# Forget-gate logits as 8-column fp32 products in four column stripes of the PE array

## Chip, cores and metric

One core of one Trainium2 chip runs the whole program. The metric is the device time of one execution in microseconds; a kernel's time is the median over several executions.

## What is computed

Two transformer-like blocks run one after the other on 512 tokens of width 2048. Only the beginning of the first block matters here: one projection `x @ w_in`, of which eight columns are the forget-gate logits, one for each head. They go through a log-sigmoid and a running sum, and the sum enters the attention logits.

```python
proj = jnp.einsum('bsd,de->bse', x, w_in[l])
(q, k, v, g_att, fg, c_b, c_c, c_h, g_conv, p_u, g_pool) = jnp.split(proj, IN_SPLITS, axis=-1)
# in forgetting_attention:
log_f = jax.nn.log_sigmoid(fg_logit.astype(jnp.float32) + b_f.astype(jnp.float32))
cum = jnp.cumsum(log_f, axis=1)
...
logits = logits + cb[..., None] - cum_k[:, :, None, :]
```

## The kernel before

x is held transposed in `feats`, as 16 planes of 128 features by 512 tokens. Every projection is done at reduced operand width (fp32r) in three products: ACT rounds each operand to a high part (`planes_hi`, `w_hi`), DVE (for planes) or POOL (for weights) subtracts it from the raw value to get the low part (`planes_lo`, `w_lo`), and PE adds hi*hi, hi*lo and lo*hi in one PSUM bank. A tile is 128 output columns; it has 16 k-steps, so 48 matmuls, and its weights come in two units of 128x1024 (8 k-steps each). Units travel through four slots (`raw[:, s]`, `w_hi[:, s]`, `w_lo[:, s]`): SP issues the load, ACT rounds (`round_unit`, L843 is its ACTIVATE), POOL subtracts (`low_part`, L396, a tensor_sub with two SBUF inputs), PE multiplies. The semaphores `hi_ready`, `lo_ready` and `unit_used` count units through these stages. Each engine runs its instructions in the order in which the program lists them, so all that follows is an order written out by hand.

The start is special. The tile that PE meets first (`project_first`, ahead of the loop over tiles) uses slots 2 and 3, and its weight low parts are made by DVE (`first_low`, L1318), not POOL. While the planes still land from memory, ACT makes one high plane after the other (`cut_hi`, L889) and DVE one low plane after the other (`cut_lo`, L1267, also a subtraction of two SBUF operands); PE waits on `planes_ready` for each. In the same loop PE computes the forget-gate logits into bank M: `fg_w` holds, for each k-step, 128 stationary columns of which columns 0 to 7 are the rounded weights and 32 to 39 their low parts, the rest zero. It lies in slots 0 and 1 of `w_hi`, which POOL clears first, so that the units of tile 1 can be rounded into these slots only when PE has passed k-step 7 (slot 0) and k-step 15 (slot 1). Two matmuls a k-step are spent on it, 32 in all, beside the 48 of the tile.

The logits then leave M: ACT adds the bias (L922, into `tmp`), DVE copies the low part (L1338), adds it (L1340), takes min(x, -x) (L1256 into `gate`), ACT does Exp and Ln (L925, L926), DVE combines and scans (L1346) into `cumT`. These ACT steps stand ahead of the rounding of tile 2's first unit in ACT's order, and POOL's low part of that unit, which PE needs for tile 2, comes after it. Tile 1 is what PE computes meanwhile.

Of the kernel before, what the change touches and what calls it, by code (L numbers as in the profile page):

```python
# [27 lines left out]
P = 128  # L28
S = 512
D = 2048  # L30
QB = S // P
KT = D // P
UNIT = 1024
UK = UNIT // P
HEADS = 8
# [33 lines left out]
X_CUTS = [(0, 1), (1, 2)] + [(k, k + 2) for k in range(2, KT, 2)]  # L69
# [46 lines left out]
def block_kernel(nc, x_t, x_rows, w_fg, stream, params, pool_w, ln1, ln2, rope_idx, rope_qk, out):  # L116
    fp32, fp32r = mybir.dt.float32, mybir.dt.float32r
    ACT, ALU, AX = mybir.ActivationFunctionType, mybir.AluOpType, mybir.AxisListType.X
# [5 lines left out]
    with ExitStack() as ctx:  # L124
# [3 lines left out]
        def sem(name):  # L128
            return ctx.enter_context(nc.semaphore(name))


        planes_hi = sb("planes_hi", [P, KT, S], fp32r)
        planes_lo = sb("planes_lo", [P, KT, S], fp32r)
        feats = sb("feats", [P, KT, S])
        raw_at = nc.sbuf_base
        raw = sb("raw", [P, 4, UNIT])
        w_hi = sb("w_hi", [P, 4, UNIT], fp32r)
# [13 lines left out]
        probs = sb("probs", [P, QB, S])  # L151
# [38 lines left out]
        states = wide[:, 1024:2048].rearrange("p (c f) -> p c f", c=QB)  # L190
        resid = [bias, probs]
        fg_raw = vN[:, 0, 0, :].rearrange("p (k c) -> p k c", k=KT)
        fg_w = w_hi[:, 0:2, :].rearrange("p s (k c) -> p (s k) c", c=P)

        def end_slot(blk, v):

# [52 lines left out]
        hi_ready, lo_ready, unit_used = sem("hi_ready"), sem("lo_ready"), sem("unit_used")  # L249
        acc_taken = sem("acc_taken")  # L250
        x_loaded = [sem(f"x_loaded{c}") for c in range(len(X_CUTS))]
        fg_loaded, fg_zeroed = sem("fg_loaded"), sem("fg_zeroed")
        first_hi, first_ready = sem("first_hi"), sem("first_ready")
        half_loaded, warm_set = sem("half_loaded"), sem("warm_set")
        par_loaded, poolw_loaded = sem("par_loaded"), sem("poolw_loaded")
# [52 lines left out]
        def _(sp):  # L308
            def load(m, s):
                sp.dma_start(raw[:, s, :], stream[at(4 * m + s - 2), :, :].rearrange("u p n -> p (u n)"))\  # L310
                    .then_inc(raw_loaded[s], 16)
# [13 lines left out]
                load_x(c)  # L325
            load(1, 0)
            load(1, 1)
            sp.wait_ge(first_ready, 3)
            load(1, 2)
            sp.wait_ge(first_ready, 4)  # L330
            load(1, 3)
            def load_next(m, s):
                sp.wait_ge(lo_ready, 4 * m + s - 7)
# [38 lines left out]
        def _(pool):  # L372
# [3 lines left out]
                step(nc.gpsimd.affine_select(out=ap, in_=ap, compare_op=op, fill=fill, base=base,  # L376
                                             pattern=pattern, channel_multiplier=mult))

            nc.gpsimd.memset(w_hi[:, 0:2, :].bitcast(fp32), 0.0).then_inc(fg_zeroed, 1)
            step(nc.gpsimd.memset(ident[:, :], 0.0))  # L380
            select(ident[:, :], ALU.not_equal, 1.0, 0, [[-1, P]], 1)
            step(nc.gpsimd.memset(causal, 0.0))
# [58 lines left out]
        def _(pe):  # L441
            def mm(o, a, b, start=True, stop=True):
                return nc.tensor.matmul(o, a, b, start=start, stop=stop)  # L443
# [4 lines left out]

            def project_first():

                pe.wait_ge(first_ready, 2)
                for e in range(KT):
                    u, k = divmod(e, UK)
                    if e in (4, UK):
                        pe.wait_ge(first_ready, 3 if e < UK else 4)
                    pe.wait_ge(planes_ready, e + 1)
                    hi, lo = w_hi[:, 2 + u, P * k:P * k + P], w_lo[:, 2 + u, P * k:P * k + P]
                    mm(M[:, :], fg_w[:, e, :], planes_hi[:, e, :], e == 0, False)
                    fg_last = mm(M[:, :], fg_w[:, e, :], planes_lo[:, e, :], False, e == KT - 1)
                    if k == UK - 1:  # L460
                        fg_last.then_inc(unit_used, 1)
                    mm(ACC[1][:, :], hi, planes_hi[:, e, :], e == 0, False)
                    mm(ACC[1][:, :], hi, planes_lo[:, e, :], False, False)
                    last = mm(ACC[1][:, :], lo, planes_hi[:, e, :], False, e == KT - 1)
                last.then_inc(unit_used, 2)

            def project(tile, acc_before, planes_cut=None, after={}):
# [88 lines left out]

            pe.wait_ge(warm_set, 1)
            for _ in range(14):
                mm(O[:, 0:P], blank, blank)
            project_first()  # L560
            pe.wait_ge(consts, 1)
            project(tile_at(T_HEAD1, 1), None)
# [264 lines left out]
        def _(act):  # L827
            step = Steps(act, act_steps)

            def signal(ins, s, value):  # L830
                ins.then_inc(s, 1)
                act.wait_ge(s, value)

            def round_first(u, cols, loaded, value):

                act.wait_ge(loaded, 16)
                signal(nc.scalar.activation(w_hi[:, 2 + u, cols], raw[:, 2 + u, cols], ACT.Copy), first_hi, value)
# [20 lines left out]
            def turn_round(tile):  # L858

                m, p = tile  # L860
                for u in range(2):
                    round_unit(m + 1, 2 * p + u)
# [29 lines left out]
            def cut_early(blk, first):  # L892
# [3 lines left out]
                for n in range(EARLY):  # L896
                    cut_hi(BACK_ORDER[blk][n], 16 + 32 * blk + n + 1)

            act.dma_start(fg_raw, w_fg).then_inc(fg_loaded, 16)
            act.dma_start(feats[:, 0:1, :], x_t[:, 0:1, :]).then_inc(x_loaded[0], 16)  # L900
            act.dma_start(par[:, :], params).then_inc(par_loaded, 16)
            act.wait_ge(warm_set, 1)
            step(nc.scalar.activation(table_of[:, :], blank[:, 0:1], ACT.Copy))
            act.wait_ge(fg_zeroed, 1)
            act.wait_ge(fg_loaded, 16)
            signal(nc.scalar.activation(fg_w[:, :, 0:HEADS], fg_raw, ACT.Copy), first_hi, 1)
            round_first(0, slice(0, S), half_loaded, 2)
            for c, (k0, k1) in enumerate(X_CUTS):
                act.wait_ge(x_loaded[c], 16)
                for k in range(k0, k1):  # L910
                    cut_hi(k, k + 1)
                if c == 2:
                    round_first(0, slice(S, UNIT), raw_loaded[2], 3)
                if c == 4:
                    round_first(1, slice(0, UNIT), raw_loaded[3], 4)
            act.wait_ge(par_loaded, 16)
            turn_round((0, 0))
            xs = tmp[0:HEADS, :]
            ls = gate[0:HEADS, :]

            act.wait_ge(unit_used, 2)
            signal(nc.scalar.activation(xs, M[0:HEADS, :], ACT.Identity,  # L922
                                        bias=par[0:HEADS, PC["b_f"]:PC["b_f"] + 1]), acc_taken, 1)
            act.wait_ge(fg_turn, 1)
# [322 lines left out]
        def _(dve):  # L1247
            V = nc.vector
            step = Steps(dve, dve_steps)

            def signal(ins, s, value):
                ins.then_inc(s, 1)
                dve.wait_ge(s, value)
# [62 lines left out]
            def first_low(u, cols, value):  # L1316
                dve.wait_ge(first_hi, value)
                signal(V.tensor_sub(w_lo[:, 2 + u, cols], raw[:, 2 + u, cols], w_hi[:, 2 + u, cols].bitcast(fp32)),  # L1318
                       first_ready, value)

            V.memset(blank, 0.0).then_inc(warm_set, 1)
            dve.wait_ge(first_hi, 1)
            signal(V.tensor_sub(fg_w[:, :, 32:32 + HEADS], fg_raw, fg_w[:, :, 0:HEADS].bitcast(fp32)), first_ready, 1)
            first_low(0, slice(0, S), 2)
            cut_lo(0, 1)
            for k in range(1, 4):
                cut_lo(k, k + 1)
            first_low(0, slice(S, UNIT), 3)
            for k in range(4, UK):
                cut_lo(k, k + 1)  # L1330
            first_low(1, slice(0, UNIT), 4)
            for k in range(UK, KT):
                cut_lo(k, k + 1)
            xs, ls = tmp[0:HEADS, :], gate[0:HEADS, :]
            fg_low = probs[0:HEADS, 1, :]

            dve.wait_ge(unit_used, 2)
            step(V.tensor_copy(fg_low, M[32:32 + HEADS, :]))  # L1338
            dve.wait_ge(acc_taken, 1)
            step(V.tensor_add(xs, xs, fg_low))  # L1340
            signal(stt(ls, xs, -1.0, xs, MULT, MIN), fg_turn, 1)
            dve.wait_ge(consts, 1)
            step(V.memset(probs[0:HEADS, 0, :], 1.0))
# [540 lines left out]
```

## Time and profile before

| | us |
|---|---|
| median of 3 runs (lowest, highest) | 1733.69 (1732.19, 1733.84) |
| the profiled execution, its time | 1734.07 |
| the profiled execution, its span | 1732.3 |
| PE busy | 1714.9 (99%) |
| DVE busy | 725.8 (42%) |
| ACT busy | 590.0 (34%) |
| POOL busy | 696.2 (40%) |

The profile is of one execution. Its span is 1.8 us shorter than its time; a step that moves the span moves the time by as much. PE is TensorE's matmul, PEld its weight load, DVE is VectorE, ACT is ScalarE, POOL is GpSimd, SP the queue that issues most loads. One fp32 matmul is two records in the trace (two passes), one fp32r matmul is one. The times of timeline rows are counted from the start of the span. A matmul's duration in a row contains its latency through the array; what it costs a busy PE is the distance to the next start.

### The profile page before, as it was taken

The page shows a single profiled execution, that of the slowest core. Times are in us where ns is not written, and L with a number is a line of the kernel's source. Part 1 is how long each engine was busy: PE and PEld are TensorE (multiplying, and loading weights), DVE is VectorE, ACT ScalarE, POOL GpSimd, SP SyncE. Part 2 cuts the span into 40 slices and gives each one's busy share as a digit, 9 for nine tenths or more (in the row PEclk, how much of TensorE's full clock was granted, in tenths as well). Part 3 has the DMA queues.
Part 4 walks back from the last instruction along what each step waited for, and adds up shares of the span by engine and source line. Part 5 has one row for each costly group of instructions (what it writes and reads, how often), then busy time and mean ns, then how long its engine had stood idle before and what let it go on. Part 6 is the DMA issues. An engine that isn't in the chain of part 4 may idle for free.

```text
span 1732.3 us, 21500 instructions
## 1 busy us (share of the span) xinstructions
PE 1714.9 (99%) x7910; PEld 1392.9 (80%) x7910; DVE 725.8 (42%) x1222; ACT 590.0 (34%) x803; POOL 696.2 (40%) x301
## 2 busy tenths in 40 slices
PE   9999999999999999999999999999999999999997
PEld 7888888888888888888888888887568787788886
DVE  4223311232211134211662744748679734465226
ACT  5433323333222224212652333423452434362120
POOL 4433333433444444445243433334236333325451
PEclk9999999999999999999999999999999999999999
DMA  6432232332332332543254443434123222227332
GB/s 223 121 91 87 90 92 92 91 92 85 92 97 97 97 98 85 171 121 98 74 196 123 124 130 91 129 109 122 49 74 98 86 73 73 85 61 267 122 97 97
DMA packets 56221, 186.15 MB, mean 107 GB/s; under 512 B 5928, under 2 KB 6184, under 8 KB 55376
## 3 DMA queue, kind: packets, MB, share of 16 engines
q1 hardware_dynamic: 46512, 160.19, 30.1%
q10 hardware_dynamic: 9632, 24.88, 4.1%
q8 instruction: 55, 0.90, 0.2%
q14 instruction: 22, 0.18, 0.0%
HBM read 176.57 MB, written 8.47 MB: 107 GB/s over the span
## 4 chain that ended last, share of the span: by engine, by line
PE 94%; DVE 3%; issue 1%; ACT 1%; DMA 1%; POOL 0%; ACTq 0%; SPq 0%; DVEq 0%; POOLq 0%
PE bank L443 92%; PE bank L447 2%; POOL w_lo L396 0%; DVE feats L1256 0%; DVE padded L1512 0%; DMA probsT<-decay_dram 0%; ACT w_hi L843 0%; DVE probs L1513 0%; DVE probs L1514 0%; DMA feats<-in_x_t 0%; DVE padded L1511 0%; DVE planes_lo L1454 0%; DVE kT L1613 0%; DVE wide L1622 0%; DVE bank L1447 0%
## 5 line engine op out<-in xcount | busy, mean ns | idle before, releaser
L396 POOL TENSOR_TENSOR w_lo<-raw,w_hi 128x1024 fp32r<-128x1024 f32 x272 | 661.6, 2434 | 994.8 <-ACT w_hi L843 994.8
L443 PE MATMUL bank<-planes_hi,w_hi 128*128 128x512 f32 (+1 forms) x1792 | 708.5, 395 | 2.0 <-DVE planes_lo L1267 1.3
L443 PE MATMUL bank<-planes_lo,w_hi 128*128 128x512 f32 (+1 forms) x1792 | 691.1, 386 | 0.0
L443 PE MATMUL bank<-planes_hi,w_lo 128*128 128x512 f32 (+1 forms) x1776 | 685.6, 386 | 0.0
L843 ACT ACTIVATE w_hi<-raw 128x1024 fp32r<-128x1024 f32 x276 | 292.7, 1060 | 975.2 <-PE bank L443 940.1
L443 PEld LDWEIGHTS bank<-planes_hi,w_hi 128*128 128x128 f32 x1792 | 337.0, 188 | 86.9 <-issue 19.2
L443 PEld LDWEIGHTS bank<-planes_lo,w_hi 128*128 128x128 f32 x1792 | 337.2, 188 | 70.4 <-issue 5.3
L443 PEld LDWEIGHTS bank<-planes_hi,w_lo 128*128 128x128 f32 x1776 | 333.8, 188 | 68.2
L443 PE MATMUL bank<-w_hi,planes_hi 128*128 128x512 f32 x480 | 187.9, 392 | 0.0
L443 PE MATMUL bank<-w_hi,planes_lo 128*128 128x512 f32 x480 | 186.8, 389 | 0.0
L443 PE MATMUL bank<-w_lo,planes_hi 128*128 128x512 f32 x480 | 186.8, 389 | 0.0
L1299 DVE COPY probsT<-bank 128x512 f32<-128x512 f32 (+1 forms) x64 | 31.4, 491 | 184.1 <-PE bank L447 182.4
L443 PEld LDWEIGHTS bank<-w_lo,planes_hi 128*128 128x128 f32 x480 | 90.1, 188 | 19.2 <-issue 0.5
L443 PEld LDWEIGHTS bank<-w_hi,planes_hi 128*128 128x128 f32 x480 | 90.1, 188 | 19.0 <-issue 0.2
L443 PEld LDWEIGHTS bank<-w_hi,planes_lo 128*128 128x128 f32 x480 | 90.1, 188 | 18.7
L1308 DVE TENSOR_TENSOR feats<-bank,gate 128x512 f32 (+1 forms) x16 | 11.1, 692 | 148.8 <-PE bank L443 148.8
L1368 DVE TENSOR_TENSOR padded<-kT,vT 128x512 f32<-128x512 f32 x4 | 9.2, 2301 | 117.6 <-ACT gate L868 117.6
L1256 DVE SCALAR_TENSOR_TENSOR feats<-probs,bank 128x512 f32<-128x512 f32 x16 | 11.0, 688 | 93.6 <-PE bank L443 93.4
L1267 DVE TENSOR_TENSOR planes_lo<-feats,planes_hi 128x512 fp32r<-128x512 f32 x48 | 43.1, 898 | 15.3 <-ACT planes_hi L889 13.7
L1256 DVE SCALAR_TENSOR_TENSOR feats<-bias,bank 128x512 f32<-128x512 f32 x16 | 11.0, 687 | 86.9 <-PE bank L443 86.5
L875 ACT ACT_TABLE_LOAD x35 | 44.9, 1283 | 1.1 <-ACT vT L868 0.5
L881 ACT ACTIVATE probs<-probs,nmax 128x128 f32<-128x128 f32 (+1 forms) x64 | 36.0, 563 | 12.1 <-DVE nmax L1286 8.0
(262 smaller groups left out, 1247.5 us busy)
## 6 DMA issues: line engine op xcount, KB each, us to landing
raw<-in_stream SPq DMA_DIRECT2D x281, 512.0 KB, 3.6
h_rows<-feats ACTq DMA_DIRECT2D x4, 1024.0 KB, 7.1
feats<-in_x_t SPq DMA_DIRECT2D x7, 512.0 KB, 8.8
out<-feats ACTq DMA_DIRECT2D x7, 512.0 KB, 2.7
rope_q<-cum_dram ACTq DMA_DIRECT2D x8, 256.0 KB, 3.1
bias<-in_x_rows ACTq DMA_DIRECT2D x2, 1024.0 KB, 6.6
probs<-in_x_rows ACTq DMA_DIRECT2D x2, 1024.0 KB, 8.8
rope_q<-decay_dram SPq DMA_DIRECT2D x8, 256.0 KB, 5.3
```

What stands on the lines that cost most here:

```text
L396: nc.gpsimd.tensor_sub(w_lo[:, s, :], raw[:, s, :], w_hi[:, s, :].bitcast(fp32)).then_inc(lo_ready, 1)
L443: return nc.tensor.matmul(o, a, b, start=start, stop=stop)
L447: return nc.tensor.transpose(o, a, ident[0:k, 0:k])
L843: signal(nc.scalar.activation(w_hi[:, s, :], raw[:, s, :], ACT.Copy), hi_ready, 4 * m + s - 3 if value is None else value)
L875: step(nc.scalar.activation(table_of[:, :], ones[:, 0:1], func))
L881: signal(nc.scalar.activation(probs[:, i, 0:n], probs[:, i, 0:n], ACT.Exp, bias=nmax[:, i:i + 1], scale=-1.0, accum_out=rowsum[:, i:i + 1] ...
L1256: return V.scalar_tensor_tensor(out=o, in0=a, scalar=scalar, in1=b, op0=op0, op1=op1)
L1267: signal(V.tensor_sub(planes_lo[:, k, :], feats[:, k, :], planes_hi[:, k, :].bitcast(fp32)), planes_ready, value)
L1299: ins = V.tensor_copy(probsT[:, j, P * j:S], B[j][:, P * j:S])
L1308: signal(V.tensor_mul(feats[:, at(tile), :].rearrange("p a n -> p (a n)"), src[:, :], gate[:, :]), feat_done, count)
L1368: step(V.tensor_mul(padded[:, 16:16 + S], kT[:, 0, :], vT[:, :]))
```

## The change

The eight columns are no longer computed from rounded parts. PE multiplies the raw fp32 weights (`fg_raw`, 128 rows by 8 columns a k-step) with the raw fp32 planes (`feats`). The four k-steps of a group of four planes write to four different column stripes of the array, partitions 0, 32, 64 and 96 of M, so each stripe collects every fourth k-step. After k-steps 3, 7, 11 and 15 PE issues one such group of four fp32 matmuls of 8 columns by 512. DVE copies the three sums at partitions 32, 64 and 96 to partition 0 and adds them to ACT's biased first sum: three copies and three additions for one of each. The padded weight array, its rounding, its low part and POOL's clearing of it go. Slots 0 and 1 of `w_hi` are free from the start, and ACT rounds tile 1's first unit ahead of the last two planes and its second unit right behind them. ACT's queue issues the load of x's first plane ahead of that of the eight columns. The semaphore values move accordingly.

```diff
@@ -190,7 +190,6 @@
         states = wide[:, 1024:2048].rearrange("p (c f) -> p c f", c=QB)
         resid = [bias, probs]
         fg_raw = vN[:, 0, 0, :].rearrange("p (k c) -> p k c", k=KT)
-        fg_w = w_hi[:, 0:2, :].rearrange("p s (k c) -> p (s k) c", c=P)
 
         def end_slot(blk, v):
 
@@ -249,7 +248,7 @@
         hi_ready, lo_ready, unit_used = sem("hi_ready"), sem("lo_ready"), sem("unit_used")
         acc_taken = sem("acc_taken")
         x_loaded = [sem(f"x_loaded{c}") for c in range(len(X_CUTS))]
-        fg_loaded, fg_zeroed = sem("fg_loaded"), sem("fg_zeroed")
+        fg_loaded, fg_done = sem("fg_loaded"), sem("fg_done")
         first_hi, first_ready = sem("first_hi"), sem("first_ready")
         half_loaded, warm_set = sem("half_loaded"), sem("warm_set")
         par_loaded, poolw_loaded = sem("par_loaded"), sem("poolw_loaded")
@@ -325,9 +324,9 @@
                 load_x(c)
             load(1, 0)
             load(1, 1)
+            sp.wait_ge(first_ready, 2)
+            load(1, 2)
             sp.wait_ge(first_ready, 3)
-            load(1, 2)
-            sp.wait_ge(first_ready, 4)
             load(1, 3)
             def load_next(m, s):
                 sp.wait_ge(lo_ready, 4 * m + s - 7)
@@ -376,7 +375,6 @@
                 step(nc.gpsimd.affine_select(out=ap, in_=ap, compare_op=op, fill=fill, base=base,
                                              pattern=pattern, channel_multiplier=mult))
 
-            nc.gpsimd.memset(w_hi[:, 0:2, :].bitcast(fp32), 0.0).then_inc(fg_zeroed, 1)
             step(nc.gpsimd.memset(ident[:, :], 0.0))
             select(ident[:, :], ALU.not_equal, 1.0, 0, [[-1, P]], 1)
             step(nc.gpsimd.memset(causal, 0.0))
@@ -448,20 +446,24 @@
 
             def project_first():
 
-                pe.wait_ge(first_ready, 2)
+                pe.wait_ge(first_ready, 1)
                 for e in range(KT):
                     u, k = divmod(e, UK)
                     if e in (4, UK):
-                        pe.wait_ge(first_ready, 3 if e < UK else 4)
+                        pe.wait_ge(first_ready, 2 if e < UK else 3)
                     pe.wait_ge(planes_ready, e + 1)
                     hi, lo = w_hi[:, 2 + u, P * k:P * k + P], w_lo[:, 2 + u, P * k:P * k + P]
-                    mm(M[:, :], fg_w[:, e, :], planes_hi[:, e, :], e == 0, False)
-                    fg_last = mm(M[:, :], fg_w[:, e, :], planes_lo[:, e, :], False, e == KT - 1)
-                    if k == UK - 1:
-                        fg_last.then_inc(unit_used, 1)
                     mm(ACC[1][:, :], hi, planes_hi[:, e, :], e == 0, False)
                     mm(ACC[1][:, :], hi, planes_lo[:, e, :], False, False)
                     last = mm(ACC[1][:, :], lo, planes_hi[:, e, :], False, e == KT - 1)
+                    if e % 4 == 3:
+                        if e == 3:
+                            pe.wait_ge(fg_loaded, 16)
+                        for j in range(4):
+                            part = mm(M[32 * j:32 * j + HEADS, :], fg_raw[:, e - 3 + j, :], feats[:, e - 3 + j, :],
+                                      e == 3, e == KT - 1)
+                            if e == KT - 1:
+                                part.then_inc(fg_done, 1)
                 last.then_inc(unit_used, 2)
 
             def project(tile, acc_before, planes_cut=None, after={}):
@@ -556,7 +558,8 @@
 
             pe.wait_ge(warm_set, 1)
             for _ in range(14):
-                mm(O[:, 0:P], blank, blank)
+                warm = mm(O[:, 0:P], blank, blank)
+            warm.then_inc(unit_used, 2)
             project_first()
             pe.wait_ge(consts, 1)
             project(tile_at(T_HEAD1, 1), None)
@@ -896,29 +899,28 @@
                 for n in range(EARLY):
                     cut_hi(BACK_ORDER[blk][n], 16 + 32 * blk + n + 1)
 
+            act.dma_start(feats[:, 0:1, :], x_t[:, 0:1, :]).then_inc(x_loaded[0], 16)
             act.dma_start(fg_raw, w_fg).then_inc(fg_loaded, 16)
-            act.dma_start(feats[:, 0:1, :], x_t[:, 0:1, :]).then_inc(x_loaded[0], 16)
             act.dma_start(par[:, :], params).then_inc(par_loaded, 16)
             act.wait_ge(warm_set, 1)
             step(nc.scalar.activation(table_of[:, :], blank[:, 0:1], ACT.Copy))
-            act.wait_ge(fg_zeroed, 1)
-            act.wait_ge(fg_loaded, 16)
-            signal(nc.scalar.activation(fg_w[:, :, 0:HEADS], fg_raw, ACT.Copy), first_hi, 1)
-            round_first(0, slice(0, S), half_loaded, 2)
+            round_first(0, slice(0, S), half_loaded, 1)
             for c, (k0, k1) in enumerate(X_CUTS):
                 act.wait_ge(x_loaded[c], 16)
                 for k in range(k0, k1):
                     cut_hi(k, k + 1)
                 if c == 2:
-                    round_first(0, slice(S, UNIT), raw_loaded[2], 3)
+                    round_first(0, slice(S, UNIT), raw_loaded[2], 2)
                 if c == 4:
-                    round_first(1, slice(0, UNIT), raw_loaded[3], 4)
+                    round_first(1, slice(0, UNIT), raw_loaded[3], 3)
+                if c == len(X_CUTS) - 2:
+                    round_unit(1, 0)
+            round_unit(1, 1)
             act.wait_ge(par_loaded, 16)
-            turn_round((0, 0))
             xs = tmp[0:HEADS, :]
             ls = gate[0:HEADS, :]
 
-            act.wait_ge(unit_used, 2)
+            act.wait_ge(fg_done, 4)
             signal(nc.scalar.activation(xs, M[0:HEADS, :], ACT.Identity,
                                         bias=par[0:HEADS, PC["b_f"]:PC["b_f"] + 1]), acc_taken, 1)
             act.wait_ge(fg_turn, 1)
@@ -1319,25 +1321,23 @@
                        first_ready, value)
 
             V.memset(blank, 0.0).then_inc(warm_set, 1)
-            dve.wait_ge(first_hi, 1)
-            signal(V.tensor_sub(fg_w[:, :, 32:32 + HEADS], fg_raw, fg_w[:, :, 0:HEADS].bitcast(fp32)), first_ready, 1)
-            first_low(0, slice(0, S), 2)
+            first_low(0, slice(0, S), 1)
             cut_lo(0, 1)
             for k in range(1, 4):
                 cut_lo(k, k + 1)
-            first_low(0, slice(S, UNIT), 3)
+            first_low(0, slice(S, UNIT), 2)
             for k in range(4, UK):
                 cut_lo(k, k + 1)
-            first_low(1, slice(0, UNIT), 4)
+            first_low(1, slice(0, UNIT), 3)
             for k in range(UK, KT):
                 cut_lo(k, k + 1)
             xs, ls = tmp[0:HEADS, :], gate[0:HEADS, :]
-            fg_low = probs[0:HEADS, 1, :]
-
-            dve.wait_ge(unit_used, 2)
-            step(V.tensor_copy(fg_low, M[32:32 + HEADS, :]))
+            dve.wait_ge(fg_done, 4)
+            for j in range(1, 4):
+                step(V.tensor_copy(probs[0:HEADS, j, :], M[32 * j:32 * j + HEADS, :]))
             dve.wait_ge(acc_taken, 1)
-            step(V.tensor_add(xs, xs, fg_low))
+            for j in range(1, 4):
+                step(V.tensor_add(xs, xs, probs[0:HEADS, j, :]))
             signal(stt(ls, xs, -1.0, xs, MULT, MIN), fg_turn, 1)
             dve.wait_ge(consts, 1)
             step(V.memset(probs[0:HEADS, 0, :], 1.0))
```

## Rows read from the trace of the kernel before

**Rows 1.** The page: the span and the busy time of each engine.
```profile
span 1732.3 us, 21500 instructions
...
PE 1714.9 (99%) x7910; PEld 1392.9 (80%) x7910; DVE 725.8 (42%) x1222; ACT 590.0 (34%) x803; POOL 696.2 (40%) x301
```

**Rows 2.** The chain that ended last, first 60 us: start, us, what.
```profile
7.55 17.73 PE bank L443 x77
```

**Rows 3.** Timeline of PE, first tiles: start, us, engine, line, operation, idle before.
```profile
25.78 0.39 PE L443 MATMUL bank<-planes_hi,w_hi 128*128 128x512 f32 x1
...
36.44 0.39 PE L443 MATMUL bank<-planes_hi,w_lo 128*128 128x512 f32 x1
37.19 0.47 PE L443 MATMUL bank<-planes_hi,w_hi 128*128 128x512 f32 x1 [0.36 <-POOL w_lo L396]
```

**Rows 4.** Timeline of ACT, first 40 us.
```profile
13.36 5.28 ACT L889 ACTIVATE planes_hi<-feats 128x512 fp32r<-128x512 f32 x8
18.68 1.06 ACT L843 ACTIVATE w_hi<-raw 128x1024 fp32r<-128x1024 f32 x1
...
26.44 0.68 ACT L922 ACTIVATE tmp<-bank,par 8x512 f32<-8x512 f32 x1
```

**Rows 5.** Timeline of DVE, first 40 us.
```profile
6.71 2.95 DVE L1267 TENSOR_TENSOR planes_lo<-feats,planes_hi 128x512 fp32r<-128x512 f32 x4
...
14.61 5.78 DVE L1267 TENSOR_TENSOR planes_lo<-feats,planes_hi 128x512 fp32r<-128x512 f32 x8
25.37 0.68 DVE L1338 COPY probs<-bank 8x512 f32<-8x512 f32 x1 [4.98 <-PE bank L443]
27.23 2.20 DVE L1340 TENSOR_TENSOR tmp<-tmp,probs 8x512 f32<-8x512 f32 x1 [1.17 <-ACT tmp L922]
29.46 0.68 DVE L1256 SCALAR_TENSOR_TENSOR gate<-tmp 8x512 f32<-8x512 f32 x1
```

**Rows 6.** Timeline of POOL, first 50 us.
```profile
19.82 2.82 POOL L396 TENSOR_TENSOR w_lo<-raw,w_hi 128x1024 fp32r<-128x1024 f32 x1 [13.77 <-ACT w_hi L843]
26.49 2.39 POOL L396 TENSOR_TENSOR w_lo<-raw,w_hi 128x1024 fp32r<-128x1024 f32 x1 [3.85 <-ACT w_hi L843]
```

**Rows 7.** Timeline of PE, fp32 products of two row halves among fp32r ones.
```profile
1225.38 0.40 PE L443 MATMUL bank<-planes_hi,w_lo 128*128 128x512 f32 x1
1225.70 1.13 PE L443 MATMUL bank<-vN,probs 64*128 64x512 f32 x4
1226.76 0.50 PE L443 MATMUL bank<-planes_hi,w_hi 128*128 128x512 f32 x1
1227.10 0.39 PE L443 MATMUL bank<-planes_lo,w_hi 128*128 128x512 f32 x1
```

**Rows 8.** Timeline of PE, fp32 products of 64 columns in two column halves (`ssd_heads`).
```profile
1008.75 0.32 PE L443 MATMUL bank<-vN,wide 128*64 128x128 f32 x1
1008.76 0.32 PE L443 MATMUL bank<-gate,wide 128*64 128x128 f32 x1
1008.91 0.27 PE L443 MATMUL bank<-vN,wide 128*64 128x128 f32 x1
```

**Rows 9.** Timeline of PE, four full-width fp32 products: 128, 256, 384, 512 columns (`head_scores`).
```profile
60.10 2.32 PE L443 MATMUL bank<-kT,qT 128*128 128x128 f32 x8
```

**Rows 10.** Timeline of DVE and POOL where low planes and low weights meet.
```profile
687.70 2.77 DVE L1267 TENSOR_TENSOR planes_lo<-feats,planes_hi 128x512 fp32r<-128x512 f32 x1
...
689.88 2.84 POOL L396 TENSOR_TENSOR w_lo<-raw,w_hi 128x1024 fp32r<-128x1024 f32 x1
...
690.50 2.76 DVE L1267 TENSOR_TENSOR planes_lo<-feats,planes_hi 128x512 fp32r<-128x512 f32 x1
```

**Rows 11.** Timeline of SP: the load of tile 1's first unit is issued.
```profile
6.61 0.44 SPq L310 DMA_DIRECT2D raw<-in_stream  x1
```

**Rows 12.** DMA issues, the same load: KB, us from issue to landing.
```profile
raw<-in_stream SPq DMA_DIRECT2D x1, 512.0 KB, 11.8
```

**Rows 13.** Windows: stretch, busy us of each engine, granted clock, DMA share, GB/s.
```profile
1208.00:1216.00 8.00, 5.12 (x22) 3.23 (x20) 7.38 (x11) 1.57 (x4) 1.36 (x1) 1.00 0.22 66
```

## The prediction

> **What bounds the kernel now.** The page comes first [rows 1]: PE is busy 1714.9 of 1732.3 us, the other engines at most 42%. So what counts is when PE gets each operand and how much it multiplies. Then the chain of waits for the first 60 us, since all of the change lies there: from 7.55 us on it is PE itself [rows 2], without a hole, to the end of the tile met first. The timeline of PE [rows 3] gives the price of one fp32r matmul: tile 1 starts at 25.78, its 48th product at 36.44, (36.44 - 25.78) / 47 = 0.227 us. Tile 2 could start at 36.44 + 0.23 = 36.67 but starts at 37.19, and the row names POOL's low part as what it waited for. So there are two limits here, not one: PE's own work up to 36.67, and the logits' chain of ACT, DVE, ACT, POOL, which ends 0.5 us later. Behind tile 2 everything waits for events that PE sets off, so a shift of tile 2's start is a shift of the end. I measure the change there.
>
> The timelines of ACT, DVE and POOL show the stretch before [rows 4 to 6]. DVE is the slowest of the three that feed PE: its low planes come each 0.72 us (5.78 / 8), ACT's high planes each 0.66 us (5.28 / 8). Planes 0 to 3 are done by 9.66, plane 8 is done at 15.33, plane 13 at 14.61 + 6 x 0.7225 = 18.95, plane 15 at 20.39. PE with five matmuls a plane (1.13 us) is slower and never waits for them after the start. With three (0.68 us) it is faster than DVE.
>
> **Removed and added on PE.** 32 fp32r matmuls go: 32 x 0.227 = 7.26 us. Four groups of four fp32 matmuls of 8 by 512 come. No row has four stripes. The nearest is a pair of fp32 products with 512 columns in two halves of the array among fp32r work [rows 7]: the slot after 1225.38 would be 1225.61; the next fp32r product starts at 1226.76 and its follower 0.34 later in place of 0.227. So one such group, with the way into the other array form and out again, costs 1.15 + 0.11 = 1.27 us. If four stripes run as two halves do, four groups cost 5.1 us. That halves run side by side is seen in the column-split products [rows 8]: two weights' products start 0.01 us apart, their second passes 0.16 us later. The other end is one after the other: four full-width fp32 products of 1280 columns in all take 2.32 - 0.16 = 2.16 us [rows 9] (0.16 is the latency in a record, 0.39 - 0.227), so 0.86 us for 512 columns, and a group costs 4 x 0.86 + 0.2 = 3.7 us. I take 1.27, since the row has the same element type, length and pair of switches. The sum of PE work alone is -7.26 + 5.1 = -2.2 us.
>
> The Trainium skill (TensorE: Matmul & The Clock Gate, "Part 3: Packing small matmuls") says that matmuls keep strict program order in start and end. An fp32 product has two passes; if these two stood together in that order, the second pass of stripe 0 would hold back stripe 1 for one pass. The rows speak against it here: both first passes lie ahead of both second ones. What it would give is the second rival.
>
> **Does PE get its planes?** Up to plane 13 ACT and DVE do what they did; the first plane may come some tenths earlier, which planes 2 and 3 (waited for from memory) take back. PE: planes 0 to 3 done at 9.66 + 0.04 + 0.68 = 10.4, group to 11.7, planes 4 to 7 to 14.4, group to 15.7, planes 8 to 11 at DVE's pace to 18.4 at most (DVE has 11 at 17.5), group to 19.7, planes 12 and 13 to 21.0.
>
> Now the moved steps. ACT has high plane 13 at 13.36 + 6 x 0.66 = 17.3 [rows 4] and then wants tile 1's first unit. Its load was issued at 6.61 and took 11.8 us [rows 11, 12]: it lands at 18.4, and ACT stands behind it, planes 14 and 15 too. Rounding takes 1.06 to 19.5; high plane 14 is there at 20.2, plane 15 at 20.9; the second unit is rounded by 22.0. POOL starts the first unit's low part at 19.6 and ends at 19.6 + 2.4 = 22.0 (2.39 when nothing disturbs it) [rows 6].
>
> Here is the point. Low planes and low weights are both subtractions of two SBUF operands, and the rows show that DVE's and POOL's exclude each other. DVE's addition at 27.23 takes 2.20 us for 8 partitions, because POOL runs from 26.49 to 28.88 [rows 5, 6]: it ends 0.55 us after POOL. Where POOL has a second operation queued, it gets in next: DVE's low plane of 687.70 ends at 690.47, POOL's operation queued at 689.88 runs to 692.72 (2.25 us after DVE let go), and DVE's next plane, started at 690.50, ends at 693.26 [rows 10]. Before, DVE had just finished plane 15 as POOL began (19.82). Now both of the last planes fall on POOL's two units:
> - low plane 14: wanted at 20.25, ends 22.0 + 0.55 = 22.55;
> - POOL's second unit, queued at about 22.05, runs until 22.55 + 2.25 = 24.8;
> - low plane 15: wanted at 22.6, ends 24.8 + 0.55 = 25.35.
>
> PE multiplies plane 14 until 23.3, waits, multiplies plane 15 from 25.4 to 26.1, and the last group until 27.35. Tile 1 starts 27.35 - 25.78 = 1.55 us later than before, in spite of 2.2 us less work: 4 us of waiting have come in.
>
> **The logits' chain to tile 2.** The last group's results are there about 0.1 us before, at 27.3; the first copy starts at 27.4, against 25.37 before. Three copies at 0.68 + 0.04 each take 2.16 [rows 5]; ACT's biased sum (0.68, [rows 4]) runs beside them, no longer behind a 1.06 us rounding. Then three additions. Each is bounded below by a subtraction of this kind left alone, 0.69, and above by the blocked one, 2.20 [rows 5]. I take 0.69 + 0.04: POOL has nothing to do then, as the next rounding stands behind this very chain on ACT. 2.19 us. The comparison with -x starts at 27.4 + 2.16 + 2.19 = 31.75, against 29.46 before: +2.3 us. From there the steps are the same, Exp, Ln, rounding, POOL's low part, so tile 2 starts at 37.19 + 2.3 = 39.5. PE is free for it at 27.35 + 10.9 = 38.25 and waits 1.2 us. On ACT the rounding of tile 2's units is queued behind the wait for the additions, and POOL behind that: this is the 2.3 us. SP's loads wait for low parts that are ready earlier than before (22.0 against 22.64), and cost nothing. POOL's clearing, one rounding (0.3 us) and one low part leave stretches in which PE waited for the first plane only. Nothing later gives the shift back.
>
> **Sum.** Profiled span 1732.3 + 2.3 = 1734.6, its time 1736.4; against the median of the three runs 1733.69 + 2.3 = 1736.0 us. A measurement of this kernel can tell about 0.2%, 3.5 us, from no change, so this is most likely within it.
>
> **Rivals.**
> 1. PE's saving arrives. If the two engines don't meet on the last planes, or only once, the last plane is ready at 21.6 to 23.3; the last group ends at 23.6 to 25.3; tile 2 starts 12.15 us later (27.35 to 39.5 above), 1.45 us earlier to 0.25 us later than before: 1732.2 to 1733.9. For it: the margin by which POOL's second unit is queued ahead of DVE's plane 15 is only 0.5 us. Even if the logits' chain cost nothing, PE would begin tile 2 at 23.6 + 10.9 = 34.5 in the best case, 2.7 us early, which is why a clear gain has little chance. Chance 0.18.
> 2. Staggered stripes. If the second pass of one stripe must end before the next stripe starts, eight passes take five slots of 0.43 us: 2.15 + 0.3 = 2.45 us a group, so 1.2 us more. The first three groups are covered by the wait for plane 14 (PE would have done plane 14 at 25.3, in time for plane 15); only the last is open: +2.3 + 1.2 = 3.5, 1737.2. Two stripes at a time (1.27 + 0.86 us) gives about the same. This is what the skill's rule would make. Chance 0.1.
> 3. The other side: the stripes run one after the other (3.7 us a group). PE: plane 3 at 10.4, then 14.1, 16.8, 20.5, 23.2, 26.9, 29.6, 33.3. It decides from about 2.5 us a group on, where the groups fill the wait for planes 14 and 15. Tile 1 starts at 33.3, 7.5 us late, the chain ends 33.3 + 12.15 = 45.45: +8.3 us, 1742.0, slower. Against it stand rows 8; for it, that no row has four streams of 512 columns at once, each with other data. Chance 0.1.
> 4. The additions meet POOL after all, each at 2.2: +4.5 on the chain, 1740.5. Chance 0.04.
>
> **Chances and range.** The forecast 0.58, by itself 1734.8 to 1737.2 (0.5 us for terms, the spread of runs on top). Of it a sixth lies beyond +3.5 us, as does half of rival 2. Faster by over 0.2%: 0.05, the tail of rival 1 and the spread. Slower: 0.1 + 0.04 + 0.05 + 0.08 = 0.27. Within: 0.68. The range takes in rivals 1 and 2 and the spread of about 0.8 us: 1731.4 to 1739.0; rivals 3 and 4 are left out.
>
> **What would show it.** In the new profile: four groups of records `bank<-feats,vN`, each about 1.2 us long; L843 starting at 18.4 with ACT idle before it; L1267's last two planes at over 2 us each, POOL's second unit at 2.75; PE idle around 21 to 25 us; three copies and three additions of 0.7 us; tile 2 at 39.5 with some 1.2 us of wait for POOL. Short last planes would make rival 1, groups of 2.4 or 3.7 us rivals 2 and 3. The granted clock stood at 1.00 through a stretch in which PE worked 5.12 of 8 us [rows 13]; should it fall during the new waits, the prediction is too low.

## The result

| | before | after |
|---|---|---|
| median (lowest to highest) of 19 executions, us | 1733.68 (1730.63 to 1735.47) | 1737.16 (1733.05 to 1738.98) |
| span of the profiled execution, us | 1732.3 | 1734.8 |
| tile 2 starts at, us | 37.19 | 39.71 |

The ratio of the times is 1.0019, 95% interval 1.0013 to 1.0026: 3.3 us longer, interval 2.3 to 4.5. The forecast was 1736.0, +2.3 us. In the profile tile 2 moved by 2.52 us and the span by 2.5. The times moved by about one microsecond more than the profile; the part on the clock takes that up.

The page after, against [rows 1]:

```profile
span 1734.8 us, 21498 instructions
...
PE 1714.3 (99%) x7910; PEld 1388.2 (80%) x7910; DVE 728.3 (42%) x1225; ACT 589.6 (34%) x802; POOL 696.0 (40%) x300
```

PE's busy time fell by 0.6 us and the span grew by 2.5, so the loss is waiting. (The saving hardly shows in the busy time: the 28 records ahead of the first plane took 6.04 us in place of 5.09 here (5.53 in a second profile of this kernel), and every record behind a wait counts its latency as busy.) The timeline of PE shows where (start, us, line, operation, idle before):

```profile
10.42 0.40 PE L441 MATMUL bank<-planes_hi,w_lo 128*128 128x512 f32 x1
10.74 1.04 PE L441 MATMUL bank<-feats,vN 128*8 128x512 f32 x8
11.72 0.50 PE L441 MATMUL bank<-planes_hi,w_hi 128*128 128x512 f32 x1
12.06 0.39 PE L441 MATMUL bank<-planes_lo,w_hi 128*128 128x512 f32 x1
...
22.77 0.50 PE L441 MATMUL bank<-planes_hi,w_hi 128*128 128x512 f32 x1 [1.52 <-DVE planes_lo L1269]
...
25.54 0.51 PE L441 MATMUL bank<-planes_hi,w_hi 128*128 128x512 f32 x1 [1.81 <-DVE planes_lo L1269]
...
27.42 0.50 PE L441 MATMUL bank<-planes_hi,w_hi 128*128 128x512 f32 x1
...
39.71 0.47 PE L441 MATMUL bank<-planes_hi,w_hi 128*128 128x512 f32 x1 [1.11 <-POOL w_lo L394]
```

One group of four stripes costs 11.72 - (10.42 + 0.227) + (0.34 - 0.227) = 1.19 us. PE is idle for 1.5 us ahead of plane 14 and for 1.8 us ahead of plane 15, starts tile 1 at 27.42 and is idle once more, 1.1 us, ahead of tile 2. By the distances from start to start, in which the latency drops out, and with 0.11 us for the slower first product behind each wait, the two planes cost 1.8 and 2.1 us. The chain of waits through that stretch (start, us, what):

```profile
6.76 11.77 DMA raw<-in_stream
...
18.64 1.07 ACT w_hi L846
19.73 0.64 ACT planes_hi L892
...
20.46 2.27 DVE planes_lo L1269
...
22.75 2.75 DVE planes_lo L1269
```

Two operations that took 0.72 us each in [rows 5] take 2.27 and 2.75. POOL's and DVE's timelines show the other side and what follows:

```profile
19.78 5.16 POOL L394 TENSOR_TENSOR w_lo<-raw,w_hi 128x1024 fp32r<-128x1024 f32 x2 [15.46 <-ACT w_hi L846]
```

```profile
27.71 2.13 DVE L1337 COPY probs<-bank 8x512 f32<-8x512 f32 x3 [2.22 <-PE bank L441]
29.87 2.11 DVE L1340 TENSOR_TENSOR tmp<-tmp,probs 8x512 f32<-8x512 f32 x3
32.01 0.68 DVE L1258 SCALAR_TENSOR_TENSOR gate<-tmp 8x512 f32<-8x512 f32 x1
```

POOL has two units in one stretch of 5.16 us, from 19.78 to 24.94; both of DVE's planes start in it, and the last one ends 0.56 us behind it. Copies and additions take 0.7 us each, and the comparison that stood at 29.46 [rows 5] stands at 32.01, +2.55.

### The profile page after: what moved, and what is told of

Its sections match the earlier page's. It is cut to its first block, busy times and chain, and to the rows that moved or that the text cites. A ratio compares the mean times of both kernels' runs of the same rounds, so it can differ in the third digit from the quotient of the medians.

```text
span 1734.8 us, 21498 instructions
## 1 busy us (share of the span) xinstructions
PE 1714.3 (99%) x7910; PEld 1388.2 (80%) x7910; DVE 728.3 (42%) x1225; ACT 589.6 (34%) x802; POOL 696.0 (40%) x300
## 4 chain that ended last, share of the span: by engine, by line
PE 93%; DVE 3%; issue 1%; DMA 1%; ACT 1%; POOL 0%; SPq 0%; DVEq 0%; ACTq 0%; POOLq 0%
PE bank L441 91%; PE bank L445 2%; DMA raw<-in_stream 1%; POOL w_lo L394 0%; DVE feats L1258 0%; DVE probs L1513 0%; DMA probsT<-decay_dram 0%; ACT w_hi L846 0%; DVE planes_lo L1269 0%; DVE probs L1514 0%; DVE padded L1512 0%; SPq L314 0%; DVE padded L1511 0%; DVE wide L1622 0%; DVE planes_lo L1454 0%
## 5 line engine op out<-in xcount | busy, mean ns | idle before, releaser
L1310 DVE TENSOR_TENSOR feats<-bank,gate 128x512 f32 (+1 forms) x16 | 11.1, 692 | 148.8 <-PE bank L441 148.8
L1269 DVE TENSOR_TENSOR planes_lo<-feats,planes_hi 128x512 fp32r<-128x512 f32 x48 | 46.7, 973 | 16.9 <-ACT planes_hi L892 15.5
```

The lines of the kernel that those rows point to most:

```text
L1269: signal(V.tensor_sub(planes_lo[:, k, :], feats[:, k, :], planes_hi[:, k, :].bitcast(fp32)), planes_ready, value)
L1310: signal(V.tensor_mul(feats[:, at(tile), :].rearrange("p a n -> p (a n)"), src[:, :], gate[:, :]), feat_done, count)
```

## Experiments

The same small instructions, PE's transposes of `cumT` (8x8, x4) in the middle of tile 2, serve as a marker: all that the change does lies ahead of them. Each ratio is against the kernel before, timed beside that kernel. The marker itself varies from profile to profile: where ACT stands behind the load of tile 1's first unit, ACT's rounding starts between 18.27 (POOL waits) and 18.64 us (after), and the marker moves with it: with filled waits the rounding is 0.26 us earlier than after and the marker 0.27.

| kernel | marker, us | span, us | median, us | ratio to before (95%) |
|---|---|---|---|---|
| before | 42.84 | 1732.3 | | |
| after | 45.35 | 1734.8 | 1737.16 | 1.0019 (1.0013 to 1.0026) |
| after, timed again | 46.03 | 1735.5 | 1737.37 | 1.0023 (1.0014 to 1.0032) |
| planes first | 41.47 | 1732.1 | 1731.41 | 0.9992 (0.9983 to 1.0001) |
| POOL waits | 41.91 | 1731.4 | 1733.14 | 0.9995 (0.9986 to 1.0005) |
| logits late | 45.11 | 1734.6 | 1736.30 | 1.0020 (1.0011 to 1.0029) |
| planes first, logits late | 39.92 | 1730.7 | 1731.11 | 0.9984 (0.9975 to 0.9994) |
| the same, again | 39.81 | 1730.4 | 1728.51 | 0.9982 (0.9973 to 0.9991) |
| before, logits late | 42.18 | 1731.6 | 1731.66 | 0.9988 (0.9979 to 0.9997) |
| the same, again | 42.41 | 1730.3 | 1733.26 | 1.0006 (0.9997 to 1.0015) |
| waits filled | 45.08 | 1733.0 | 1736.35 | 1.0013 (1.0003 to 1.0022) |
| one stripe | 49.96 | 1739.4 | 1741.22 | 1.0044 (1.0030 to 1.0058) |

**Planes first.** ACT rounds tile 1's first unit behind the last planes.

```diff
             for c, (k0, k1) in enumerate(X_CUTS):
...
-                if c == len(X_CUTS) - 2:
-                    round_unit(1, 0)
+            round_unit(1, 0)
             round_unit(1, 1)
```

> The changed kernel, but ACT rounds tile 1's first unit behind the last two planes, not ahead of them. Theory (DVE's low planes 14 and 15 each stand behind one of POOL's low units): POOL begins only when DVE has the planes, both L1269 rows are back at 0.7 us, the last plane is ready at 20.5, the last group ends at 23.7, tile 1 starts 3.7 us earlier than in the changed kernel (27.4) and, as the logits' chain is unchanged (12.3 us from tile 1's start to tile 2's), tile 2 starts at 36.0 in place of 39.7. Time 3.7 us below the changed kernel and 1.2 us below the kernel before. Rival (the groups in stripes themselves, or PE's switches of array form, cost the time): last group still ends after 26 us, and the time stays at the changed kernel's.

DVE's eight last planes run through undisturbed, and PE waits only for the logits' chain, at tile 2:

```profile
14.74 5.78 DVE L1268 TENSOR_TENSOR planes_lo<-feats,planes_hi 128x512 fp32r<-128x512 f32 x8
```

```profile
35.84 0.47 PE L441 MATMUL bank<-planes_hi,w_hi 128*128 128x512 f32 x1 [1.12 <-POOL w_lo L394]
```

The marker is 3.88 us earlier than after (expected 3.7) and the time back at or below that of the kernel before. The groups in stripes are in there unchanged, so they don't cost it. But the move takes away two things at once: the meeting with POOL and ACT's stand behind the load.

**POOL waits.** The load's stand stays, only the meeting goes.

```diff
+            pool.wait_ge(planes_ready, KT)
             low_parts(1, m_misc - 1)
```

> The changed kernel with one wait added: POOL starts its first low unit only when DVE has made all 16 low planes. ACT's order, with its stand behind the load that lands at 18.5, stays. Theory (it is the meeting of DVE and POOL): low planes 14 and 15 take 0.7 us each and end at 21.9, the last group ends at 23.8, tile 1 starts at 24.5 when POOL has its unit; POOL's second unit then blocks the first addition (1.5 us more), tile 2 starts at 36.4, 3.3 us earlier than in the changed kernel. Rival (ACT's stand behind the load is the cause, and POOL only happens to run): plane 15 is still not ready before 25 us and tile 2 starts at 39.7 or later.

```profile
18.27 1.06 ACT L847 ACTIVATE w_hi<-raw 128x1024 fp32r<-128x1024 f32 x1 [1.19 <-DMA raw<-in_stream]
```

```profile
20.10 1.42 DVE L1270 TENSOR_TENSOR planes_lo<-feats,planes_hi 128x512 fp32r<-128x512 f32 x2 [1.40 <-ACT planes_hi L893]
23.73 2.13 DVE L1338 COPY probs<-bank 8x512 f32<-8x512 f32 x3 [2.21 <-PE bank L442]
25.89 2.63 DVE L1341 TENSOR_TENSOR tmp<-tmp,probs 8x512 f32<-8x512 f32 x3
```

ACT still stands 1.19 us behind the load, as in the changed kernel, and yet the two planes take 1.42 us together. The marker is 3.44 us earlier than after (expected 3.3), 0.4 us short of the run before; 0.37 us of the 3.44 are the load, which landed that much earlier in this profile. So it is the meeting of DVE and POOL; delaying POOL by a wait gives back nearly all. The small rest is 0.5 us on the additions (1.5 had been expected), the first of which meets POOL's second unit. PE's wait for POOL at tile 1 costs nothing at tile 2, where PE still has to wait for the logits' chain.

**Logits late.** The other term, the longer chain, taken off tile 2's path.

```diff
-            act.wait_ge(fg_turn, 1)
-            step(nc.scalar.activation(ls, ls, ACT.Exp))
-            signal(nc.scalar.activation(ls, ls, ACT.Ln, bias=1.0), fg_turn, 2)
             for j, dst in enumerate((qT[:, :], kT[:, 0, :], vT[:, :])):
                 t = tile_at(T_HEAD1, j)
                 turn_round(t)
                 take(t, dst, T_HEAD1 + j + 1)
+                if j == 0:
+                    act.wait_ge(fg_turn, 1)
+                    step(nc.scalar.activation(ls, ls, ACT.Exp))
+                    signal(nc.scalar.activation(ls, ls, ACT.Ln, bias=1.0), fg_turn, 2)
```

> The changed kernel, but ACT rounds tile 2's two units and takes tile 0's result before it waits for DVE's additions; Exp and Ln of the logits come behind them. Theory (the rest of the loss is the longer chain of logits ahead of tile 2's rounding): tile 2 starts as soon as PE has done tile 1, 38.45 in place of 39.71, though the additions now meet POOL's units and take over 2 us each. Time 1.3 us below the changed kernel. Rival (it is only PE's work and the late planes): no change of tile 2's start by more than 0.2 us.

The wait ahead of tile 2 is gone, but the marker moved by 0.24 us only, not 1.3. The reason for the difference is in the timeline of PE and in the windows (stretch, busy us of PE, PEld, DVE, ACT, POOL, granted clock, DMA share, GB/s):

```profile
25.26 0.79 PE L441 MATMUL bank<-planes_hi,w_hi 128*128 128x512 f32 x1 [1.80 <-DVE planes_lo L1270]
...
26.83 1.79 PE L441 MATMUL bank<-feats,vN 128*8 128x512 f32 x8
28.55 0.50 PE L441 MATMUL bank<-planes_hi,w_hi 128*128 128x512 f32 x1
```

```profile
20.00:25.00 5.00, 1.98 (x8) 0.98 (x6) 4.78 (x2) 1.77 (x3) 4.63 (x2) 1.00 0.49 190
25.00:28.40 3.40, 3.14 (x11) 0.95 (x11) 0.20 (x1) 0.00 (x0) 0.00 (x0) 0.50 0.55 169
28.40:30.00 1.60, 1.60 (x10) 1.24 (x7) 1.12 (x2) 1.11 (x2) 0.00 (x0) 1.00 0.00 0
```

In this execution the granted clock was 0.50 (1.2 GHz) from 25.0 to 28.4, right behind 5 us in which PE was busy for 1.98 us. The last group took 1.79 us, not 1.04, and tile 1 started 1.13 us later than in the changed kernel's profile. The expectation had no room for that. From tile 1's start to the marker, behind all of this, there are 45.11 - 28.55 = 16.56 us, against 45.35 - 27.42 = 17.93 in the changed kernel: the move is worth 1.37 us there, and 1.26 had been expected. Against the second profile of the changed kernel, in which the clock fell likewise, the gain at the marker is 46.03 - 45.11 = 0.92 us, and the medians give 0.9 to 1.1. It is smaller there because part of the fall is hidden in the very wait that the move takes away: PE, slower up to tile 2, then waits 0.48 us for POOL and not 1.11.

```profile
40.41 0.47 PE L441 MATMUL bank<-planes_hi,w_hi 128*128 128x512 f32 x1 [0.48 <-POOL w_lo L394]
```

**The clock.** Is that fall the microsecond by which times and profile differ? The changed kernel was timed again beside one that keeps PE at work in the two waits.

> The changed kernel itself, timed beside the others of this call. In its 19 executions the longest (1738 to 1739 us) had a mean granted clock of 0.994 to 0.995 and the shortest (1733 to 1735) one of 0.997 to 0.998. Theory (in part of its executions the clock falls to 0.50 for 3.4 us while PE waits for planes 14 and 15, as the profile of the run with the logits late shows): times in steps of about 1.7 us again, median some 3.5 us over the kernel before, of which 2.5 us are in the profile. Rival: one cluster at 2.5 us over.

```diff
+                    for _ in range({14: 7, 15: 8}.get(e, 0)):
+                        mm(O[:, 0:P], blank, blank)
                     pe.wait_ge(planes_ready, e + 1)
```

> The changed kernel with products of no use in PE's two waits: 7 fp32 products of 128 columns (0.22 us each) ahead of the wait for plane 14 and 8 ahead of that for plane 15, into a bank that nobody reads then. The waits end when they did, tile 1 at 27.4 and tile 2 at 39.7. Theory (the excess over the profile's 2.5 us is the clock): no run shows the additional 3.4 us at half clock, the mean granted clock is 0.996 to 0.998, the median falls by about 1 us against the changed kernel of this call, to 2.5 us over the kernel before. Rival (the clock has nothing to do with the waits): the median stays.

Windows of the changed kernel's second profile, then of the kernel with filled waits:

```profile
24.00:26.00 2.00, 0.66 (x3) 0.49 (x3) 1.29 (x1) 0.00 (x0) 0.74 (x1) 1.00 0.84 225
26.00:28.00 2.00, 2.00 (x10) 0.12 (x8) 0.00 (x0) 0.00 (x0) 0.00 (x0) 0.53 0.60 223
28.00:30.00 2.00, 2.00 (x9) 1.54 (x6) 1.54 (x3) 0.68 (x1) 0.00 (x0) 0.62 0.04 16
```

```profile
20.00:22.00 2.00, 2.00 (x16) 1.83 (x15) 1.80 (x1) 1.79 (x3) 1.98 (x2) 1.00 0.60 236
22.00:24.00 2.00, 2.00 (x16) 1.75 (x15) 1.97 (x2) 0.00 (x0) 2.00 (x1) 1.00 0.26 72
24.00:26.00 2.00, 1.97 (x15) 1.56 (x13) 1.24 (x1) 0.00 (x0) 0.68 (x1) 1.00 0.64 207
26.00:28.00 2.00, 2.00 (x14) 0.82 (x13) 0.55 (x1) 0.53 (x1) 0.00 (x0) 1.00 0.76 244
```

The same program shows the fall in one profile and not in the other. Timed again, the changed kernel's median was 3.6 us over the kernel before (expected 3.5), with times from 1735.2 to 1739.3. Over its 30 executions the mean granted clock and the time go together, roughly: those at 0.994 took 1739.0 to 1739.3 us, those at 0.997 and 0.998 took 1733.1 to 1736.5, those at 0.996 anything from 1733.4 to 1738.0. With products of no use in the waits none of 11 executions is below 0.996, the median is 1.0 us lower, at 1736.35, and the ratio is 1.0013 against 1.0023. The fall is shown in two profiles (the changed kernel's second, logits late) and its absence with filled waits in one. That it makes up the microsecond in the times is likely, not shown: the two intervals overlap, and the mean clock doesn't say where the clock fell. There is a second place, near 1215 us, where it falls in some executions (last section), and the filled kernel's profile has no fall there either.

**One stripe.** What the array stripes are worth.

```diff
-                            part = mm(M[32 * j:32 * j + HEADS, :], fg_raw[:, e - 3 + j, :], feats[:, e - 3 + j, :],
-                                      e == 3, e == KT - 1)
+                            part = mm(M[0:HEADS, :], fg_raw[:, e - 3 + j, :], feats[:, e - 3 + j, :],
+                                      e - 3 + j == 0, e - 3 + j == KT - 1)
...
-            for j in range(1, 4):
-                step(V.tensor_copy(probs[0:HEADS, j, :], M[32 * j:32 * j + HEADS, :]))
...
-            for j in range(1, 4):
-                step(V.tensor_add(xs, xs, probs[0:HEADS, j, :]))
```

> All 16 fp32 products of 8 columns go to the one stripe at partition 0 and add up in PSUM; DVE's three copies and three additions go. Theory (stripes run side by side, 1.18 us a group; in one stripe eight passes of 0.43 us follow each other, 3.65 us a group): PE becomes the bound, groups end at 14.3, 20.6, 27.0 and 33.4, tile 1 starts at 33.4, the logits are ready at once, tile 2 starts at 44.3, when PE is free: 4.6 us over the changed kernel, 7.1 us over the kernel before. Rival (stripes gain little, as all read full 128 rows): groups hardly longer than 1.2 us, and the time below the changed kernel by the 4.2 us of copies and additions, less PE's 1.1 us wait as far as it reaches.

```profile
10.13 0.40 PE L441 MATMUL bank<-planes_hi,w_lo 128*128 128x512 f32 x1
10.46 3.60 PE L441 MATMUL bank<-feats,vN 128*8 128x512 f32 x8
13.99 0.50 PE L441 MATMUL bank<-planes_hi,w_hi 128*128 128x512 f32 x1
```

A group takes 3.60 us where four stripes take 1.04, and the marker is 4.61 us later than after, as expected (4.6). So the four stripes do run side by side, and the third rival's price of 3.7 us a group was about that of a single stripe.

**Both moves.** What is the change worth with both obstacles gone?

> Both: planes ahead of tile 1's units on ACT, and tile 2's rounding ahead of the logits' Exp and Ln. Theory: PE runs without a wait from tile 1 into tile 2, tile 1 at 23.7, tile 2 at 34.6: 5.1 us below the changed kernel, 2.5 us below the kernel before, which is the whole of PE's saving in products. Rival (a further wait hides behind these two): tile 2 starts at 35.5 or later, or a wait comes up at tile 2's second half or at tile 3, because the additions blocked by POOL delay Exp and Ln and with them tile 3's rounding.

The marker is at 39.92, 2.9 us ahead of the kernel before (expected 2.5) and 5.4 ahead of the changed one (expected 5.1); the DVE chain of the logits is slow now (three additions in 6.16 us, as they meet POOL's units) and nobody waits for it. The logits' move alone, put on the kernel before:

> The kernel before with the one move of the logits-late run: ACT rounds tile 2's units and takes tile 0's result before it waits for the additions. Theory (the chain of logits held tile 2 back by 0.5 us there too): tile 2 starts at 36.7 in place of 37.2, 0.5 us less, which the times can hardly tell; so of the 2.8 us that both moves bring over the kernel before, over 2 us are PE's saving in products. Rival (the move alone gives it): 2 us or more below the kernel before.

The marker moved by 0.66 us, as expected, but the median was 2.1 us lower, which left open whether the logits' move was all of the gain. So both were timed once more, on one chip:

> The kernel with both moves once more, on one chip with the kernel before that has only the logits moved. In the traces PE's small transposes in the middle of tile 2 come at 39.9 us here, at 42.2 there and at 42.8 in the kernel before. Theory (PE's saving in products is worth its 2.2 us once nothing holds PE back): 2.2 us below the other kernel of this call, 2.8 below the kernel before. Rival (what was gained is the logits' move alone): both kernels of this call within 1 us of each other.

> The kernel before with the logits moved, once more. Theory: 0.6 us below the kernel before, as in its trace; the 2 us that the median of the first timing showed are the half-clock stretches, which came in fewer of its executions than in those of the kernel before. Rival: 2 us below again.

This time the logits' move alone is at 1.0006 (0.9997 to 1.0015) and both together at 0.9982 (0.9973 to 0.9991): medians of 1733.26 and 1728.51, markers of 42.41 and 39.81. The 2 us of the first timing did not come again, and the expected 0.6 us didn't show in the times either; at the marker the move gave 0.66 and 0.43. The clock went the way of the times: the median of the mean granted clocks was 0.998 against 0.997 for the kernel before in the first timing, and 0.997 against 0.998 in the second. That the clock is the whole reason is not shown. The 4.8 us between the two medians are more than the traces bear out: six executions with both moves took 1728.0 to 1728.5 us and five 1731.0 to 1732.5, so one execution decides in which group the median stands. The saving in PE's products is real, 2.3 and 2.6 us at the marker in the two pairs of profiles, once no wait takes its place. This version is a little faster than the kernel before, by 3.1 us (1.6 to 4.7) in this last timing, and so than the changed one.

## Why the prediction was right, point by point

- *A group of four stripes costs 1.27 us, by the nearest row.* 1.19. All four first passes lie ahead of the four second ones, the order that [rows 8] had. A stretch of the changed kernel's timeline that ends at 11.1 us has the first four of the eight records, and only them:

```profile
10.74 0.62 PE L441 MATMUL bank<-feats,vN 128*8 128x512 f32 x4
```

- *Staggered passes, the second rival,* would have made 2.45 us a group. They are not there. The Trainium skill's rule of strict program order (TensorE: Matmul & The Clock Gate, "Part 3: Packing small matmuls") does not hold, by this trace, for the two passes of one fp32 product as a pair.
- *ACT stands behind the load until 18.4.* It stood until 18.64, with 1.19 us of idle time named after the DMA.
- *Both last planes meet POOL.* Forecast ends 22.55 and 25.35, measured 22.73 and 25.50; tile 1 was forecast at 27.35 and started at 27.42. The rule was taken from [rows 10], who is queued gets in next, and it held: DVE ended 0.56 us after POOL (0.55 there), POOL's second unit 2.21 us after DVE (2.25). Two runs took the meeting away in two ways, and both gave back 3.4 to 3.9 us. One reading beside it was wrong: in the kernel before DVE had not finished plane 15 as POOL began at 19.82. It ended at 20.39, and POOL's unit lasted 2.82 us in place of 2.39 [rows 5, 6]. There too the two met, but DVE was in first, so it was POOL that stood, and nobody needed its unit yet.
- *The logits' chain is 2.3 us late.* +2.55 at the comparison with -x. It began at 27.71, 0.3 us after the forecast's 27.4; copies and additions took 4.30 us up to the comparison, 4.35 had been set. No addition met POOL, the fourth rival: the three took 2.11 us.
- *PE waits 1.2 us ahead of tile 2.* 1.1.
- *Nothing later gives it back.* The span without the marker is 1689.5 before and after.

What was left out is the clock. The prediction let the clock pass with [rows 13], a stretch at 1.00 with a PE wait in it. That stretch ended too early. The windows of the kernel before show a fall just behind a wait of 3 us there, and so does the timeline of PE, where four records of 64 rows by 512 columns take 1.82 us and not 1.13 [rows 7]:

```profile
1210.00:1215.00 5.00, 3.12 (x14) 1.86 (x13) 4.60 (x9) 0.01 (x1) 0.00 (x0) 1.00 0.36 105
1215.00:1220.00 5.00, 3.85 (x9) 2.04 (x10) 2.61 (x5) 2.93 (x5) 0.00 (x0) 0.66 0.00 0
```

```profile
1216.15 1.82 PE L443 MATMUL bank<-vN,probs 64*128 64x512 f32 x4 [3.03 <-ACT bias L1172]
```

So the price of a few microseconds of waiting was there to be read. The prediction did name a fall as what would make it too low, but gave it no place in the sum. It is the likely reason why the times moved by 3.3 to 4.0 us (the two ratios) and not 2.3 to 2.5, and by that the result lies in the upper part of the range and at the edge of the 0.2% within which it was most expected (1.0019, interval 1.0013 to 1.0026).

Two sums of the prediction don't come out as written. A sixth of 0.58 is 0.10, where 0.08 was added to the chance of slower. And rival 2 with the spread gives 1737.2 + 0.8 = 1738.0 as the upper end of the range, not 1739.0; the result, 1737.16, lies below both.

## What to carry to other kernels

Work taken off the bounding engine is only worth what its next operand allows: here 7.26 - 4 x 1.19 = 2.5 us of products were saved, and, from start to start, 3.9 us came in at planes 14 and 15, 0.7 us more ahead of tile 2 and 0.4 us at the first planes, which a faster PE has to wait for as well. Most of it came in because a rounding moved ahead of the last planes started POOL while DVE still had two subtractions to make. When a step is moved, follow what it sets free on a third engine and what that engine shares with those that feed the bound. And read the clock in the windows behind a wait, not only in the one around it.

## What the runs showed of the hardware that had not been expected

- Behind two waits of 1.5 and 1.8 us with 0.7 us of products between them TensorE's granted clock fell to 0.50 (1.2 GHz) for 3.4 us in the second profile of the changed kernel and in that of logits late, and not in the first profile of the changed kernel. It cost PE 28.55 - (25.26 + 1.88) = 1.4 us in logits late, where 1.88 us is the same stretch at 1.00 in the changed kernel's first profile (27.42 - 25.54).
- The same holds for the 3 us wait near 1215 us, which all kernels here have. Span less marker is 1687.9 us in the two profiles in which the clock stayed up there (waits filled; before with logits late, again), 1689.4 to 1689.5 where it was down for 3.4 us, and 1690.6 to 1690.8 where it was down for twice that (planes first; both moves, twice). In planes first the windows of 5 us from 1210, 1215 and 1220 stand at 0.88, 0.50 and 0.94, which makes (0.6 + 2.5 + 0.3) / 0.5 = 6.8 us at half clock. This is a good part of the spread of 4 us among executions of one kernel, and the reason why the marker tells differences that the times can't.
- Four column stripes of 8 columns, each with its own 512 columns of moving fp32 data over all 128 rows, run at (3.60 - 0.16) / (1.04 - 0.16) = 3.9 times the speed of one stripe (0.16 us is the latency in a row), or at 3.2 times with the switches of array form: 13.99 - (10.13 + 0.227) + 0.11 = 3.75 us against 1.19.
